# A mixture-of-experts loop on 64 token slots instead of 128, with extra blocks for experts that have more

## What is computed

```python
def _moe(h, router_w, router_b, w1, w3, w2):
    s = jax.nn.sigmoid((h @ router_w).astype(jnp.float32))       # N x 32
    sb = s + router_b
    ...                                                          # best group of 8 experts, its top 2
    _, eidx = lax.top_k(jnp.where(emask, sb, -jnp.inf), K)
    wsel = jnp.take_along_axis(s, eidx, axis=1)
    wsel = wsel / jnp.sum(wsel, axis=-1, keepdims=True)
    ...                                                          # pairs sorted by expert
    def expert_block(args):
        xe, e = args
        return (jax.nn.silu(xe @ w1[e]) * (xe @ w3[e])) @ w2[e]  # 1024 -> 512 -> 1024
```

## Time and profile before

| | |
|---|---|
| three runs | 3682.4, 3682.86 and 3685.11 us, median 3682.86 |
| profiled execution | 3683.92 us, span 3682.1 us |
| mean granted clock | 0.927 |
| TensorE busy | 3181.0 us, 86% |
| VectorE busy | 2032.7 us, 55% |
| ScalarE busy | 1539.1 us, 42% |
| DMA | 615.88 MB, mean 167 GB/s |
| experts, first layer | 1473.47 to 2076.52 us |
| experts, second layer | 3159.02 to 3647.22 us |

### The profile page before, as it was taken

One profiled execution on the slowest core, in us unless ns is written; L12 is line 12 of the kernel. 1 busy time (PEld: TensorE's weight loads), 2 busy tenths in 40 slices (PEclk: granted clock), 3 DMA queues, 4 the chain that ended last, 5 costly groups with the idle time before them and its releaser, 6 DMA issues. The chain is left out here.

```text
span 3682.1 us, 46697 instructions
## 1 busy us (share of the span) xinstructions
PE 3181.0 (86%) x16830; PEld 2629.1 (71%) x16830; DVE 2032.7 (55%) x2961; ACT 1539.1 (42%) x2164; POOL 0.2 (0%) x4
## 2 busy tenths in 40 slices
PE   8987999887886976999999878788768876799998
PEld 6676766565775763888888737776567866699997
DVE  3454645464454732766666345555464444688884
ACT  3222245332332231666666333334333333577773
POOL 0000000000000000000000000000000000000000
PEclk8998999988997978999999988899989988899999
DMA  4111411041211420899999302241052223699994
GB/s 184 69 46 69 168 52 36 21 177 69 69 58 41 176 99 0 330 338 340 338 341 340 128 35 103 99 178 52 23 206 81 81 79 132 263 422 423 422 422 182
DMA packets 76175, 615.88 MB, mean 167 GB/s; under 512 B 9694, under 2 KB 11680, under 8 KB 13472
## 3 DMA queue, kind: packets, MB, share of 16 engines
q1 hardware_dynamic: 76064, 614.43, 43.4%
HBM read 613.34 MB, written 1.05 MB: 167 GB/s over the span
## 5 line engine op out<-in xcount | busy, mean ns | idle before, releaser
L167 PE MATMUL ps<-rounded,rounded 128*128 128x256 f32 (+1 forms) x1936 | 676.3, 349 | 115.1 <-DVE rounded L158 94.3
L168 PE MATMUL ps<-rounded,rounded 128*128 128x256 f32 (+1 forms) x1936 | 665.7, 344 | 0.0
L169 PE MATMUL ps<-rounded,rounded 128*128 128x256 f32 (+1 forms) x1936 | 663.7, 343 | 0.0
L158 DVE TENSOR_TENSOR rounded<-low_arena,rounded 128x1024 fp32r<-128x1024 f32 (+3 forms) x302 | 359.2, 1228 | 338.4 <-ACT rounded L154 338.4
L167 PEld LDWEIGHTS ps<-rounded,rounded 128*128 128x128 f32 x1936 | 385.6, 199 | 163.6 <-DVE rounded L158 98.1
L143 PE MATMUL ps<-high_arena 128*128 128x256 f32 (+4 forms) x1488 | 437.0, 453 | 73.0 <-ACT low_arena L1616 16.3
L143 PEld LDWEIGHTS ps<-low_arena,high_arena 128*128 128x128 f32 x4096 | 467.0, 192 | 7.4 <-issue 2.4
L143 PE MATMUL ps<-low_arena,high_arena 128*128 128x128 f32 x4096 | 467.7, 275 | 2.0 <-ACT low_arena L2220 1.3
L154 ACT ACTIVATE rounded<-low_arena 128x1024 fp32r<-128x1024 f32 (+3 forms) x302 | 306.5, 1057 | 353.4 <-PE ps L169 274.2
L143 PEld LDWEIGHTS ps<-high_arena 128*128 128x128 f32 x1488 | 289.5, 208 | 208.7 <-issue 115.6
L2242 DVE TENSOR_TENSOR rounded<-high_arena,rounded 128x1024 fp32r<-128x1024 f32 x256 | 313.3, 1225 | 188.1 <-ACT rounded L2202 167.9
(11 more groups left out here) (317 smaller groups left out, 3625.1 us busy)
## 6 DMA issues: line engine op xcount, KB each, us to landing
high_arena<-in_e_w SPq DMA_DIRECT2D x248, 1024.0 KB, 7.4
high_arena<-in_e_w SPq DMA_DIRECT2D x68, 2048.0 KB, 9.2
low_arena<-in_d_wm SPq DMA_DIRECT2D x48, 1024.0 KB, 4.8
high_arena<-in_d_modlater SPq DMA_DIRECT2D x40, 1024.0 KB, 7.0
low_arena<-in_d_wml SPq DMA_DIRECT2D x32, 1024.0 KB, 4.9
low_arena<-in_d_wh SPq DMA_DIRECT2D x16, 1536.0 KB, 6.7
low_arena<-in_d_wa SPq DMA_DIRECT2D x16, 1536.0 KB, 6.7
low_arena<-in_d_wo SPq DMA_DIRECT2D x8, 1024.0 KB, 4.8
```

The costliest lines, as they stand in the source:

```text
L158: return v.tensor_tensor(lo, raw, hi.bitcast(F32), ALU.subtract)
L167: pe.matmul(out, l_hi, r_hi, start=(k == 0), stop=False)
L168: pe.matmul(out, l_lo, r_hi, start=False, stop=False)
L169: last = pe.matmul(out, l_hi, r_lo, start=False, stop=(k == n - 1))
```

## The change

The first layer's stage works on 64 slots too, and the two forms of the expert loop become one. In the first layer it has four pairs of split buffers (`homes`, `NB`), in the second eight as before.

- `S` is 64 in both layers. In the first, `n_over` becomes 15 instead of 7, and `nb` takes six operations behind the first instead of two.
- The up products of the first layer are the two of the second layer's form, 32 for an expert, and the sum of the halves comes behind them.
- With four pairs of buffers granules 4 to 7 of an expert (`OWN`) are split while its products run, granules 0 and 1 of the next (`PRE`) ahead of the gate, and granules 2 and 3 (`MID`) behind the tanh on ScalarE and behind the gate on VectorE.
- In the extra blocks, of both layers, each matrix has a semaphore of its own (`o_in1`, `o_in3`, `o_in2`). The next `w1` is loaded when the products with `w1` are done (`o_half`), the next `w3` after those with `w3` (`o_up`), the next `w2` after the down products (`o_down`). TensorE waits for each matrix where it needs it.

On the inputs that the reference draws, its router gives the experts of the first layer at most 92, 76, 67 and 53 pairs, and those of the second at most 53.

```diff
-    S = SLOT if ns == 2 else SLOT // 2
+    S = SLOT // 2
     n_over = (A - 1) // S
...
-        def up_products(pe, s, bank):
-            for i, w in enumerate((w1[s], w3[s])):
-                for f in range(4):
-                    last = accumulate(pe, K.ps[:, bank + i, f * S:f * S + S], lambda k: w[:, k, f * P:f * P + P], lambda k: xg[s][:, k, :], KC)
+        def up_products(pe, s, bank, i):
+            w = (w1, w3)[i][s]
+            for f in range(4):
+                last = accumulate(pe, K.ps[:, bank + i, f * S:f * S + S], lambda k: w[:, k, f * P:f * P + P], lambda k: xg[s][:, k, :], KC)
             return last
...
-                        sp.wait_ge(o_down, b)
-                        for dst, src in expert_tiles(K, l, e, 1):
-                            sp.dma_start(dst, src).then_inc(o_in, 16)
+                        for (dst, src), used, landed in zip(expert_tiles(K, l, e, 1), (o_half, o_up, o_down), (o_in1, o_in3, o_in2)):
+                            sp.wait_ge(used, b)
+                            sp.dma_start(dst, src).then_inc(landed, 16)
...
-                        pe.wait_ge(o_in, b * 48 + 48)
+                        pe.wait_ge(o_in1, b * 16 + 16)
                         pe.wait_ge(o_taken, b + 1)
-                        up_products(pe, 1, 2).then_inc(o_up, 1)
+                        up_products(pe, 1, 2, 0).then_inc(o_half, 1)
+                        pe.wait_ge(o_in3, b * 16 + 16)
+                        up_products(pe, 1, 2, 1).then_inc(o_up, 1)
                         pe.wait_ge(o_gated, b + 1)
+                        pe.wait_ge(o_in2, b * 16 + 16)
                         pe.wait_ge(o_out, b)
                         down_products(pe, 1, 6).then_inc(o_down, 1)
...
-        if ns == 2:
...
-                                pe.matmul(out, x_hi[:, k, :], w_hi[i % AHEAD][:, j, :], start=(k == 0), stop=False)
-                                pe.matmul(out, x_lo[:, k, :], w_hi[i % AHEAD][:, j, :], start=False, stop=False)
-                                last = pe.matmul(out, x_hi[:, k, :], w_lo[i % AHEAD][:, j, :], start=False, stop=(k == KC - 1))
...
-        else:
+        with nc.Block() as block:
...
+            homes = [152 + 8 * q for q in range(4)] + ([52, 60, 88, 96] if ns == 1 else [])
+            NB = len(homes)
+            PRE = range(EARLY // 2) if ns == 2 else range(EARLY)
+            MID, POST = (range(2, 4), range(0)) if ns == 2 else (range(EARLY, EARLY + 1), range(EARLY + 1, GR))
+            OWN = range(NB, GR)
...
+                            pe.matmul(out, x, w_hi[i % NB][:, j, :], start=(k == 0), stop=False)
+                            last = pe.matmul(out, x, w_lo[i % NB][:, j, :], start=False, stop=(k == KC - 1))
...
+                    if free:
+                        act.wait_ge(w_used, e * GR + (i + 1 - NB))
...
+                def step(e, s, first=False, more=True):
+                    for i in OWN:
+                        round_(e, i)
+                    if more:
+                        for i in PRE:
+                            round_(e + 1, i)
+                    act.wait_ge(w_used, e * GR + GR)
...
+                    act.activation(low, K.ps[S:2 * S, 0:2, :], ACT.Copy).then_inc(half_copied, 1)
...
+                    act.activation(tanh, u[:, 0, :], ACT.Tanh, scale=0.5).then_inc(tanh_done, 1)
+                    if ns == 2 and more:
+                        for i in MID:
+                            round_(e + 1, i)
+                    if not first:
+                        store(e - 1, 1 - s)
```

More of the change, by code:

```diff
@@ L1835, in stage_moe @@
              "h_copied", "onehot", "gathered", "sorted_", "starts_turned", "starts_ready",
-             "o_in", "o_taken", "o_up", "o_tanh", "o_gated", "o_down", "o_out", "o_chain",
+             "o_in1", "o_in3", "o_in2", "o_half", "o_taken", "o_up", "o_tanh", "o_gated", "o_down", "o_out", "o_chain",
              "raw_in0", "raw_in1", "raw_in2", "raw_in3", "w_rounded", "w_split", "w_used", "x_rounded", "x_split",
@@ L1842, in stage_moe @@
                                h_copied, onehot, gathered, sorted_, starts_turned, starts_ready,
-                               o_in, o_taken, o_up, o_tanh, o_gated, o_down, o_out, o_chain,
+                               o_in1, o_in3, o_in2, o_half, o_taken, o_up, o_tanh, o_gated, o_down, o_out, o_chain,
                                raw_in0, raw_in1, raw_in2, raw_in3, w_rounded, w_split, w_used, x_rounded, x_split,
```

453 lines of the change are left out of this document (151 added, 302 removed).

## The result

The kernel before takes 3683.41 us (median of four runs, 3682.4 to 3685.11), the changed one 3720.45 us (four runs, 3717.0 to 3723.39). The ratio is 1.010, with a 95% interval of 1.0082 to 1.0117. The forecast was 3723 us, in a range of 3706 to 3750. The profiled execution of the changed kernel has a span of 3721.6 us, 39.5 more than before, and a mean granted clock of 0.907 instead of 0.927.

What follows compares the result with a forecast made beforehand. TensorE was taken to bound the first expert loop alone, TensorE and DMA the second. 3683.9 - 98 + 138 + 0.8 = 3724.7, less 1.1 against the median and with copies not counted: 3723 us, range 3706 to 3750.

Steps and rivals of the forecast that it cites:

- The first layer's loop: First layer's expert loop: 64 slots save up to 114.8 us, four buffers take back 18, a shorter first gate gives 1: -98.
- the stall: First layer's up products: with four buffer pairs they end 0.57 us later than in the second layer, 18 us over 31 experts.
- The blocks: Ahead of the first layer's expert loop: three extra blocks run at the half clock, +138 in all (bounds 79 to 145).
- The term for the idle trips: Loop of extra blocks: five more idle trips at 0.7 are 3.7 us, most issued under the last products, so 1 us.
- rival 4: Extra blocks of the first layer: none runs, the pair counts being other than worked out; 3589 us, chance 2%.
- Loading each matrix early: Extra blocks: later matrices land behind running products, so it costs and saves nothing beyond the first wait, 8.3 us together.
- Counting: Block counting: four more VectorE operations, 0.42 us for two, on a chain for which TensorE waits: +0.8 us.
- rival 2: First layer's expert loop: four buffers stall it, at 1.39 us a remainder 23 us longer; 3746 us, chance 8%.
- rival 3: First layer's expert loop: loads set the pace at 340 GB/s, 18.5 us an expert, no gain; 3821 us, chance 2%.
- The reason for the half clock: Extra blocks: TensorE starts at 0.54 after waiting, and 64 columns resemble 32, so half clock throughout, 13.86 us a matrix.
- Rival 1: Extra blocks: the clock rises, so three cost 70.3 us instead of 129.2; 3664 us, chance 10% (4% for a partial rise).

Runs made afterwards that it cites:

- The release experiment: Against the changed kernel, each granule's two high-part products come first and release that buffer by their own semaphore; 3706.52 us, ratio 1.0064.

## Why the prediction was right, and where its reason was not

- **The first layer's loop, forecast -98.** Measured -96.6 (506.4 against 603.0); the 0.06 that an expert takes longer than forecast, over 31 experts 1.9, more than cover the 1.4 between them. The steps of the stall came as forecast: ScalarE starts 1.22 after the first up product (1.20), VectorE at 2.31 (2.27) and its six remainders take 6.90, 1.15 each; the up products last 8.02 (7.96), the expert 15.52 (15.46). The gate ends at 1700.27, 2.5 ahead of the transposes. The release experiment shows that the stall is this chain.
- **The blocks, forecast +138.** Measured 149.5 - 12.8 = +136.7. The first matrix came 8.2 after its issue, where the forecast had 7.5 and 0.8 ahead of it for the expert's number; 64 instructions take 13.7 to 13.9 (13.86), a gate 1.38 (1.5). Three blocks, as counted. By the medians the run without them is 133 shorter. The term for the idle trips (1 us, at 0.7 a trip) and rival 4's 3.7 rest on a rough price: rival 4 would have had eight more idle trips, not five. Eight trips fewer gave 5.0 and four fewer 2.9, so 0.6 to 0.7 each.
- **Loading each matrix early, forecast to leave only the first wait.** No block after the first waits for a matrix; undone, it costs 45.
- **Counting, forecast +0.8.** Six operations take 1.32 instead of 0.42, and TensorE waits 15.04 instead of 14.14:

```profile
1397.57 1.32 DVE L2029 SCALAR_TENSOR_TENSOR high_arena<-high_arena 128x32 f32<-128x32 f32 x6
...
1402.02 0.59 PE L1940 MATMUL ps<-ident,high_arena 128*1 128x128 f32 x2 [15.04 <-DVE high_arena L2044]
```

- **The rivals on the loop.** The period is 15.52, not the 16.2 of rival 2, and the loads run at 399 GB/s without a wait of TensorE for them, where rival 3 had 340. The Trainium skill's 358 GB/s (DMA: Bandwidth & Descriptors, "Specifications") is passed here too.
- **The rest.** -96.6 + 136.7 is 40.1 of the 39.5 that the span grew; the parts outside, the stretch to the end of the gather (-1.5) and that behind the loop (+1.0), differ by no more than runs do.
- **The reason for the half clock was right for the block's start and wrong for its width.** I put 64 columns beside the 32 of the earlier trace rows, which pull the clock down from 1.00. The experiments show three kinds, over the stretches that ran here: 32 columns pull it down while they run, 64 columns keep whichever level they find, 128 columns raise it. What priced the blocks at 13.9 us a matrix was the level at which they began, 0.54 after the idle time; the start stood in the prediction, but as a side argument. The stop in each gate, which drops the clock where it's up, stood there only as 1.5 us. The number was thus right in part by luck: with the clock raised ahead of the blocks the same argument would still have given 0.50 throughout, and that kernel takes 16.6 us less. Rival 1's "once at the full clock 64 columns might hold it" was true, and its condition, the clock up at the start, was not given. The Trainium skill, TensorE: Matmul & The Clock Gate, "Why this matters for your kernels", asks for a TensorE that is kept continuously busy: the filled stops agree (21.55 us at 1.00), the changed kernel's 27.57 us without a gap at 0.50 do not.

What is not settled: the first products of the expert loops run at 0.50 for some 5 us behind the wait for VectorE (in the changed kernel up to 1613.9, where a product's duration falls from 0.63 to 0.40); no run tried to fill that wait. That ahead of the first matrix, over 8 us, is still there too: it was filled with products, not shortened.

## What to carry to other kernels

A rare path that is entered more often has to be priced at the clock it will run at: look at what TensorE did just before it, at how wide its products are and at its stops, since in these runs a change of any one of them changed the level. Where narrow products start cold, wider or additional ones can be cheaper than the plain ones: 128 columns saved 52 us of the 137 that the blocks cost, and idle waits filled with products 58. Halving a tile's slots is worth its saving in the loop only after the overflow it creates has been counted on the real inputs and multiplied by its cost.

## What the runs showed that I had not expected

Full-float32 products of 128x64 come 0.112 us apart at 1.00 and 0.215 at 0.50, and neither level changes while they run: 41.22 us without a gap leave the clock at 0.50, and 21.55 us leave it at 1.00. A stop of 1.38 us between 64-column products dropped the clock (0.84 and then 0.50), one of 2.13 us between 128-column products did not (1.00 through it). Eight idle trips fewer of a loop over a condition shortened the wait behind it by 5.0 us, 0.6 each, and four fewer by 2.9 in the layer in which no block ever runs. Much of such a trip is its test: in the run without blocks, whose trips have none, 15 trips left a wait of 12.26 us, and seven with the test left 12.81.
